# High parts first: each piece of weights is begun before its low part is cut, with a half-size Fourier step and modulation weights taken in pairs

## The reference

```python
def hybrid_layer(x, ...):                      # twice
    h = rms_norm(x, g_mix_pre)
    z = jnp.matmul(h, w_in)                    # 1024 x 3200
    ...                                        # retention, dilated attention, spatial gating
    x = x + rms_norm(jnp.matmul(y, w_out), g_mix_post)
    h = rms_norm(x, g_ffn_pre)
    gate, up = jnp.split(jnp.matmul(h, w_gate_up), [FFN_HIDDEN], axis=-1)
    f = jnp.matmul(jax.nn.silu(gate) * up, w_down)
    return x + rms_norm(f, g_ffn_post)

def fourier_mix(u):                            # even layer, both streams, 4 groups of 128 channels
    f = jnp.fft.fft2(u.reshape(b, n, 4, 128), axes=(1, 3), norm='ortho')
    return f.real.reshape(b, n, 512)

    # second network, per layer: modulation of both streams from the two vectors c and c_ctx
    mod_l = silu_c @ w_mod[l] + b_mod[l]       # 1024 x 3072
    mod_c = silu_cc @ w_mod[l] + b_mod[l]
```

## Time and profile before

| what | value |
|---|---|
| median of 3 runs | 1123.51 us |
| the profiled execution's own time | 1121.75 us |
| its span in the trace | 1119.9 us |
| PE busy | 1086.1 us, 97% of the span, 5974 matmul records |
| DVE busy | 683.9 us, 61% |
| ACT busy | 554.7 us, 50% |
| POOL busy | 77.2 us, 7% |
| loaded from memory | 168.39 MB, 151 GB/s over the span |

### The profile page before, as it was taken

How to read it: one execution, slowest core, us unless ns; L and a number is a source line. 1 busy time by engine, 2 the same in 40 slices (tenths; PEclk the granted TensorE clock), 3 DMA queues, 4 the chain that set the end, 5 groups by cost and what they waited for, 6 DMA issues and landing times.

```text
span 1119.9 us, 15597 instructions
## 1 busy us (share of the span) xinstructions
PE 1086.1 (97%) x5974; PEld 883.6 (79%) x5974; DVE 683.9 (61%) x1198; ACT 554.7 (50%) x999; POOL 77.2 (7%) x94
## 2 busy tenths in 40 slices
PE   7999999999999999999999999999998999999997
PEld 5889776688886988776688778889796678889785
DVE  5986665566545786575566547523256753876664
ACT  5654364455435554364455445334235642534772
POOL 1000110000002000110000000001000002021040
PEclk9999999999999999999999999999999999999999
DMA  9644576665666744486876485223211012443001
GB/s 300 218 141 151 173 241 192 219 211 186 188 188 203 242 139 152 143 280 211 256 235 183 153 323 153 73 87 107 75 58 57 1 57 57 132 142 122 2 1 38
DMA packets 109716, 170.46 MB, mean 152 GB/s; under 512 B 7229, under 2 KB 70730, under 8 KB 109386
## 3 DMA queue, kind: packets, MB, share of 16 engines
q1 hardware_dynamic: 107668, 161.95, 45.8%
q0 software_dynamic: 1440, 6.10, 1.6%
q10 hardware_dynamic: 534, 1.41, 0.3%
HBM read 168.39 MB, written 1.05 MB: 151 GB/s over the span
## 4 chain that ended last, share of the span: by engine, by line
PE 84%; DVE 8%; ACT 4%; issue 3%; DMA 1%; POOL 0%; SPq 0%; DVEq 0%; POOLq 0%; ACTq 0%
PE PS L477 16%; PE PS L478 15%; PE PS L479 15%; PE PS L2997 4%; PE PS L2998 4%; PE PS L2999 4%; PE PS L977 3%; PE PS L1810 1%; DVE low L450 1%; PE PS L941 1%; PE PS L942 1%; PE PS L943 1%; PE PS L1484 1%; ACT high L440 1%; PE PS L1798 1%
## 5 line engine op out<-in xcount | busy, mean ns | idle before, releaser
L450 DVE TENSOR_TENSOR low<-raw,high 128x1024 fp32r<-128x1024 f32 (+3 forms) x182 | 202.2, 1116 | 190.8 <-ACT high L440 189.9
L477 PE MATMUL PS<-high,hT_high 128*128 128x512 f32 (+2 forms) x796 | 308.0, 387 | 4.3 <-DVE low L450 2.0
L478 PE MATMUL PS<-low,hT_high 128*128 128x512 f32 (+2 forms) x796 | 299.5, 376 | 0.0
L479 PE MATMUL PS<-high,hT_low 128*128 128x512 f32 (+2 forms) x796 | 299.4, 376 | 0.0
L440 ACT ACTIVATE high<-raw 128x1024 fp32r<-128x1024 f32 (+3 forms) x186 | 179.6, 972 | 221.1 <-PE PS L479 123.4
L477 PEld LDWEIGHTS PS<-high,hT_high 128*128 128x128 f32 x796 | 150.6, 189 | 49.5 <-issue 15.0
L453 DVE SCALAR_TENSOR_TENSOR low<-raw,vec_cols,high 128x512 fp32r<-128x512 f32 x176 | 124.2, 747 | 75.3 <-ACT high L443 75.2
L479 PEld LDWEIGHTS PS<-high,hT_low 128*128 128x128 f32 x796 | 150.5, 189 | 24.2
L478 PEld LDWEIGHTS PS<-low,hT_high 128*128 128x128 f32 x796 | 150.8, 189 | 21.7
L443 ACT ACTIVATE high<-raw,vec_cols 128x512 fp32r<-128x512 f32 x176 | 117.1, 714 | 73.9 <-PE PS L479 38.5
L2997 PE MATMUL PS<-high,fT_high 128*128 128x512 f32 x176 | 70.4, 400 | 0.0
(11 more groups left out here) (377 smaller groups left out, 1602.0 us busy)
## 6 DMA issues: line engine op xcount, KB each, us to landing
raw<-w_gate_up SPq DMA_DIRECT2D x176, 256.0 KB
raw<-w_mod SPq DMA_DIRECT2D x48, 512.0 KB
raw<-w_down SPq DMA_DIRECT2D x44, 512.0 KB
raw<-w_in SPq DMA_DIRECT2D x56, 384.0 KB
raw<-o_w_in SPq DMA_DIRECT2D x20, 512.0 KB
raw<-w_out SPq DMA_DIRECT2D x16, 512.0 KB
raw<-e_w_in SPq DMA_DIRECT2D x12, 512.0 KB
raw<-w_in SPq DMA_DIRECT2D x8, 512.0 KB
```

Of the source, the lines that this page charges most:

```text
L450: last = e.tensor_tensor(g.low, g.raw, g.high.bitcast(F32), ALU.subtract)
L477: e.matmul(bank, xh[:, k, tokens], g.high[:, i, :], start=first and i == 0, stop=False)
L478: e.matmul(bank, xh[:, k, tokens], g.low[:, i, :], start=False, stop=False)
L479: done = e.matmul(bank, xl[:, k, tokens], g.high[:, i, :], start=False, stop=last and i == len(g.rows) - 1)
```

## The change

1. `products`, `out_products` and `down`: PE begins a piece when its high part is there (`high_ready`). For each block of rows it runs the two matmuls that need the high part alone, and after both blocks, behind a wait for the low part in tile 0, the matmuls with the low part. Two places that were ordered by the old wait get a wait of their own (`ffn_gained`).
2. The eight single modulation pieces of each layer come in four pairs, behind the pieces 1 and 3 of the chunks 2 and 4.
3. The Fourier step computes 129 of the 256 frequencies. The others are the same numbers in reverse order (for the sines with the other sign), so each copy from PSUM is now two, the second of them reading backwards, and the channels' table has a third block with the other sign.
4. Steps 5, 1 and 2 of the rotary tables all run on DVE before its first cut of the second chunk.
5. `hT_high` and `hT_low` are allocated earlier in SBUF, and `half_power` is 24 columns wide instead of 16.

```diff
-    parts["dft_tokens"] = by_tile(np.concatenate([np.cos(turn), np.sin(turn)], 1))
+    half = slice(0, SEQ // 2 + 1)
+    parts["dft_tokens"] = by_tile(np.concatenate([np.cos(turn)[:, half], np.sin(turn)[:, half]], 1))
...
-        MOD_AT = {(2, h): (0, h) for h in range(4)} | {(4, h): (1, h) for h in range(4)}
+        MOD_AT = {(2, 1): (0, 0), (2, 3): (0, 2), (4, 1): (1, 0), (4, 3): (1, 2)}
...
+        def high_ready(e, g):
+            e.wait_ge(highs_cut, g.cut + 1)
...
             for i, k in enumerate(g.rows):
                 e.matmul(bank, xh[:, k, tokens], g.high[:, i, :], start=first and i == 0, stop=False)
-                e.matmul(bank, xh[:, k, tokens], g.low[:, i, :], start=False, stop=False)
-                done = e.matmul(bank, xl[:, k, tokens], g.high[:, i, :], start=False,
+                e.matmul(bank, xl[:, k, tokens], g.high[:, i, :], start=False, stop=False)
+            if t == 0:
+                low_ready(e, g)
+            for i, k in enumerate(g.rows):
+                done = e.matmul(bank, xh[:, k, tokens], g.low[:, i, :], start=False,
                                 stop=last and i == len(g.rows) - 1)
             return done
...
             for h, g in enumerate(granules):
-                low_ready(e, g)
+                high_ready(e, g)
...
-                    last = e.matmul(PS[:, 4 + i % 4, :], z_late[:, NT * s + t, g * P:(g + 1) * P],
+                    last = e.matmul(PS[:, 4 + i % 4, 0:2 * FH], z_late[:, NT * s + t, g * P:(g + 1) * P],
...
-                copy(e, mine, fourier_T[:, i, :], PS[:, 4 + i % 4, :]).then_inc(mine.sem, mine.mark(f"fourier{i}"))
+                halves = PS[:, 4 + i % 4, 0:2 * FH].rearrange("p (c n) -> p c n", c=2)
+                to = fourier_T[:, i, :].rearrange("p (c n) -> p c n", c=2)
+                copy(e, mine, to[:, :, 0:P], halves[:, :, 0:P])
+                copy(e, mine, to[:, :, P:SEQ], halves[:, :, P:0:-1]).then_inc(mine.sem, mine.mark(f"fourier{i}"))
...
-        EARLY = {0: 5, 1: 1, 2: 2, 4: 3, 6: 4}
+        EARLY = {0: (5, 1, 2), 4: (3,), 6: (4,)}
...
             def free_z(c, t):
-                if c == 2:
+                if c == 1 and layer:
+                    e.wait_ge(dve.sem, dve.value(f"ffn_gained{t}0", layer=layer - 1))
+                elif c == 2:
                     e.wait_ge(act.sem, act.value(f"zg{t}"))
...
-                        mod_rows_pe(e, 0, of, slice(n, n + 1))
+                        mod_rows_pe(e, 0, of, slice(n, n + 2))
```

More of the change, by code:

```diff
@@ L93, in late_constants @@
     turn = 2 * np.pi * ((n[:, None] * n[None, :]) % SEQ) / SEQ
-    parts["dft_tokens"] = by_tile(np.concatenate([np.cos(turn), np.sin(turn)], 1))
+    half = slice(0, SEQ // 2 + 1)
+    parts["dft_tokens"] = by_tile(np.concatenate([np.cos(turn)[:, half], np.sin(turn)[:, half]], 1))
     turn = 2 * np.pi * ((p[:, None] * p[None, :]) % P) / P
-    parts["dft_channels"] = np.concatenate([np.cos(turn), -np.sin(turn)], 1) / np.sqrt(SEQ * P)
+    parts["dft_channels"] = np.concatenate([np.cos(turn), -np.sin(turn), np.sin(turn)], 1) / np.sqrt(SEQ * P)
     for name, width in (("mla", MR), ("gqa", HD)):
@@ L191, in program @@
         low = [sb(f"low{i}", [P, SLOT], F32R) for i in range(CUT)]
+        hT_high = sb("hT_high", [P, DK, SEQ], F32R)
+        hT_low = sb("hT_low", [P, DK, SEQ], F32R)
         consts = sb("consts", [P, a["const_early"].shape[1]])
@@ L211, in program @@
         modT = sb("modT", [P, DEPTH * 24, 2])
-        half_power = sb("half_power", [P, 16])
+        half_power = sb("half_power", [P, 24])
         cosf = sb("cosf", [P, NT, HD])
@@ L364, in add_gu @@
                         of, n = MOD_AT[c, h]
-                        add_mod(layer, 0, (of,), PAIRS[n:n + 1])
+                        add_mod(layer, 0, (of,), PAIRS[n:n + 2])
                     w_gu[layer].add_split(a["w_gate_up"][layer], rows, c * SEQ, SEQ, pre_gain(V_FFN, layer, rows))
@@ L941, in out_products @@
                 e.matmul(bank, xh[:, tokens], g.high[:, i, :], start=first and i == 0, stop=False)
-                e.matmul(bank, xh[:, tokens], g.low[:, i, :], start=False, stop=False)
-                done = e.matmul(bank, xl[:, tokens], g.high[:, i, :], start=False, stop=last and i == len(g.rows) - 1)
+                e.matmul(bank, xl[:, tokens], g.high[:, i, :], start=False, stop=False)
+            if t == 0:
+                low_ready(e, g)
+            for i, k in enumerate(g.rows):
+                done = e.matmul(bank, y_operand(k)[0][:, tokens], g.low[:, i, :], start=False, stop=last and i == len(g.rows) - 1)
             return done
@@ L1472, in program @@
                    for s, banks in enumerate(banks2))
+        FH = SEQ // 2 + 1
         def fourier_first_pe(e):
@@ L1505, in fourier_second_pe @@
                     for part in range(2):
+                        of = part * (1 + t % NT)
                         rows = slice(part * SEQ + t % NT * P, part * SEQ + (t % NT + 1) * P)
                         last = e.matmul(PS[:, F_BANKS[t], g * P:(g + 1) * P], fourier_T[:, 4 * s + g, rows],
-                                        channels[:, part * P:(part + 1) * P], start=part == 0, stop=part == 1)
+                                        channels[:, of * P:(of + 1) * P], start=part == 0, stop=part == 1)
                 last.then_inc(pe.sem, pe.mark(f"fourier_mixed{t}"))
@@ L2805, in dve_layer @@
                     where.section = "pre"
-                    early_dve(e, EARLY[s])
+                    for step in EARLY[s]:
+                        early_dve(e, step)
                     where.section = "layer"
@@ L2997, in down @@
                     e.matmul(bank, fT_high[:, n, tokens], g.high[:, 0, cols], start=n == 0, stop=False)
-                    e.matmul(bank, fT_high[:, n, tokens], g.low[:, 0, cols], start=False, stop=False)
-                    last = e.matmul(bank, fT_low[:, n, tokens], g.high[:, 0, cols], start=False, stop=n == FK - 1)
+                    e.matmul(bank, fT_low[:, n, tokens], g.high[:, 0, cols], start=False, stop=False)
+                    if t == 0 and j == 0:
+                        low_ready(e, g)
+                    last = e.matmul(bank, fT_high[:, n, tokens], g.low[:, 0, cols], start=False, stop=n == FK - 1)
                     if n == FK - 1 and (t == 0 or j == 0):
@@ L3033, in pe_layer @@
                 g = e_in[0].granules
+                e.wait_ge(dve.sem, dve.value("ffn_gained00"))
                 first_pieces_pe(e, 2, False, g[0:2])
```

7 lines of the change are left out of this document (2 added, 5 removed).

## The result

The changed kernel takes 1092.49 us (median of 4 runs, 1089.97 to 1093.7), the kernel before 1123.36 beside it: a ratio of 0.9727, 95% interval 0.9705 to 0.9748. That is 30.9 us less. In the profiled execution (1092.06 us, span 1090.3) the difference to that of before is 29.7 us.

What follows compares the result with a forecast made beforehand. PE was taken to bound the kernel, busy 1086.1 of 1119.9 us. The terms 9.3 + 6.6 + 1.5 + 0.45 + 1.3 = 19.2 us, taken from 1123.5, gave 1104 us, with a range of 1100 to 1109.

Steps and rivals of the forecast that it cites:

- part 5: SBUF places and wider half_power: forecast to gain nothing, only 8 more columns of a memset during PE's first load wait.
- Modulation: 16 single pieces become 8 pairs; each pair's second piece is free on PE, 9.3 us less.
- Fourier: First Fourier product: 32 records shrink from 512 to 258 columns, 6.6 us less, doubled copies hidden behind PE.
- High part first: PE begins pieces sooner: 0.9 us at the start, twice 0.75 before w_gate_up, 0.4 to 0.5 before layer 1's w_in.
- Tables earlier: ACT's 0.44 us wait for the angles goes; rotated queries come sooner, PE's 2.71 us wait shrinks to about 2.3.
- The slower one: Rival: the new wait inside each of 274 pieces costs a 0.10 us restart, 27 us, giving 1131; chance 0.05.
- The loads: Rival: paired pieces delay w_gate_up's loads, 1.2 us back at each of four places, 5 us, giving 1109; chance 0.1.
- The high part first does something: Judges the rival that it does nothing because DVE is late: 2 to 3 us less gain, 1107; chance 0.12.
- The clock staying up: Rival: the clock stays up at 47 us, after PE's wait for the queries; 1.3 us more gain, 1103; chance 0.2.

Runs made afterwards that it cites:

- run 1: Kernel before with the two SBUF layout edits alone (hT_high and hT_low declared first, half_power 24 wide); 1111.46 us, ratio 0.9901.
- run 6: Kernel before with the modulation pieces in pairs alone; 1113.5 us, ratio 0.9915.
- run 15: Kernel before with the new order within a piece alone (high part's products first), all else old; 1119.84 us, ratio 0.9978.
- run 8: Changed kernel with the rotary tables at their old places; 1093.67 us, ratio 0.9741.
- run 2: Changed kernel with the old SBUF layout (hT_high and hT_low where they stood, half_power 16 wide); 1105.0 us, ratio 0.9844.
- run 5: Changed kernel with the old order within a piece (high, low, high with hT_low); 1094.93 us, ratio 0.9751.
- run 7: Kernel before with Fourier's first product for half the frequencies alone, copies reversed; 1114.91 us, ratio 0.9931.
- run 12: Changed kernel, but the first four pieces of the program begin only when their low part is there too; 1091.17 us, ratio 0.9721.

## Why the prediction was wrong

**The step that failed is part 5**, "Places in SBUF and the wider `half_power`: nothing". It measured 10.9 us (run 1), against a miss of 11.7. I had priced the addresses at nothing without a row for it: all the trace of before could show was steps of 233 ns with one layout. No rival held it and the range had no room for it. An honest bound was in reach. The earlier trace rows gives a step of 0.24 to 0.23, and the prediction had read 0.43 at 1.2 GHz from the earlier trace rows, which is about one column per cycle and halves to 0.213 at 2.4 GHz. So the steps could fall by up to 0.02, which over 2,590 matmuls is 52 us. For a change that moves two tensors with no stated use, this should have opened the low end.

Point by point:
1. **Modulation**, 9.3: measured 9.1 (run 6). Eight records cost 0.99 us, as read, and layer 0 gains the 4.7 that this gives. In layer 1 the loads took 2.0 back in run 6's trace, a cost that the sum had left to a rival.
2. **Fourier**, 6.6: measured 7.7 (6.4 to 9.2), 6.8 by the two groups' busy times. The copies stay hidden. The prediction says that each engine gets a result every fourth record; it is every eighth, and the 1.76 us that it goes on with is right.
3. **High part first**, 2.85: measured 2.4 and 3.2. The mechanism held at the boundaries, 0.95 and 0.94 for 2 x 0.75, and 0.73 for 0.45. At the start it failed (0.9 forecast). PE began 1.1 to 2.1 us sooner and was stopped at 17.8 to 18.8 by what it needed next. I had looked at what PE waits for first and not at what stands behind those four pieces. That is the turn of the vectors, which waits for hT_low, and the turn of ws_rows, which waits for a load.
4. **Tables earlier**, 0.44: the changed kernel reaches the queries at 46.37 and 45.78 (its two profiles), before at 46.20. The wait there is 2.6 us in both, and not the 2.3 of the forecast; with the new order but the old tables it is 3.04 (run 15) and 3.14 (run 8), so in the traces the early tables do shorten it by 0.4 to 0.5. Run 8 gives 1.2 in time with intervals that overlap those of the changed kernel, so neither 0.44 nor nothing is excluded.

With 9.1, 7.7, 2.4, 1.2 and 10.9 the parts sum to 31.3, against 30.9 measured for all together. Each is known to 1.2 us at best and mostly to 1.5, so it is luck that they meet within 0.4; what they do show is that nothing of 5 us or more is left over.

**The rivals.** The slower one is refuted: a wait in the middle of each piece costs nothing where it is met, since the steps of run 2 (new order, old layout) are 233 ns as before. The loads gave part back at one place, w_gate_up of layer 1. There ACT stands for a load, DVE's cuts and then the gate f come late, and PE waits 0.90 us where before it had no wait:

```profile
524.35 1.34 ACT L444 ACTIVATE high<-raw,vec_cols 128x512 fp32r<-128x512 f32 x2 [5.66 <-DMA raw<-w_gate_up]
```

```profile
525.71 2.91 DVE L454 SCALAR_TENSOR_TENSOR low<-raw,vec_cols,high 128x512 fp32r<-128x512 f32 x4 [6.21 <-ACT high L444]
```

```profile
530.19 0.65 PE L2993 MATMUL PS<-consts,f 128*128 128x128 f32 x4 [0.90 <-DVE f L2841]
```

(Timelines of ACT, DVE and PE of the changed kernel.) So that rival holds at one of its four places, for about 1 us of its 5 in the changed kernel and for 2.0 in run 6, which has no new order. Run 15, with the old modulation, has 0.24 there, and run 1, with nothing but the layout, 0.43, so a faster PE alone brings some of it. The high part first does something: the interval of run 15 ends at 0.9989. The clock staying up is a matter of each execution; it came in 4 of the 10 profiles of which I read this stretch (before, the changed kernel twice, and runs 1, 5, 6, 7, 8, 12, 15), for 0.8 us in run 15, less than the 1.3 of part 4.

## What to carry to other kernels

- For float32 products in which each matmul of 512 columns has a weight load of its own, put the stationary and the moving tensor at the same rest by 256 bytes within the partition, and measure it, since with 256 columns the steps of run 1 are 2 ns longer. A small pad between two declarations can be worth 1% (run 1). A change that only moves buffers or widens a small tensor needs a term of its own in the sum, with the steps' distance from the pure stream as its bound.
- Starting an engine earlier pays only up to the next thing that it must wait for. Follow its queue past the first wait.
- Parts measured one by one that add up (31.3 for 30.9) show that no large term is left over. They don't show that each part is free of give and take inside it; for that a trace was laid beside another, matmul by matmul.

## What the runs showed of the hardware

- Two operands in unlike places cost 5 to 6 ns of each 512-column step (233 for 227 to 228 ns). With 384 and with 256 columns no such rule is seen.
- Even alike, the step is 227 ns. The Trainium skill (TensorE: Matmul & The Clock Gate, "Back-to-back issue gap") gives about 216 ns for an isolated matmul of 512 columns and 131 in a stream with weight loads; this trace agrees with neither for its split products, and comes nearer to the first.
- After a wait of 2.6 to 3.1 us the clock may stay at 2.4 GHz (runs 5, 6, 7 and 15) or go to 1.2 for some 3 us (before, the changed kernel twice, runs 1 and 12; some 7 us in run 8), with the same work ahead of it in run 6 as in before. A fall where PE is busy costs about half its length: 1.7 us of 3.4 at 850 us in run 6.
